# A fused two-block forward pass: five residual turns done as products with a diagonal

## What is computed

```python
def _rmsnorm(x, g):
    y = x * lax.rsqrt(jnp.mean(x * x, axis=-1, keepdims=True) + RMS_EPS)
    return y * g

for i in range(2):                                     # first block
    hn = _rmsnorm(x, norm1[i])
    mix, q_mem = mixer[i](hn, ...)
    x = x + concat([mix, mem_attention(q_mem, ...)]) @ w_o[i]
    x = x + swiglu(_rmsnorm(x, norm2[i]), w_ffn_in[i], w_ffn_out[i])
x = _rmsnorm(x, final_norm)
h = rmsnorm(x, mix_pre_g)                              # second block
merged = ...                                           # from h @ w_in
x = x + rmsnorm(merged @ w_out, mix_post_g)
x = x + rmsnorm(swiglu(rmsnorm(x, ffn_pre_g), ...), ffn_post_g)
```

## Time and profile before

| | |
|---|---|
| runs, us | 1379.44 median, 1378.86 to 1386.27 |
| the profiled execution, us | 1386.25 |
| its span from first to last instruction, us | 1384.5 |
| PE busy | 1260.3 us, 91% of the span |
| DVE busy | 746.5 us, 54% |
| ACT busy | 601.2 us, 43% |
| mean granted PE clock | 0.945 of full speed |
| DMA moved | 184.59 MB, mean 133 GB/s |

### The profile page before, as it was taken

One profiled execution on the slowest core, in us unless ns is written; L12 is line 12 of the kernel. 1 busy time (PEld: TensorE's weight loads), 2 busy tenths in 40 slices (PEclk: granted clock), 3 DMA queues, 4 the chain that ended last, 5 costly groups with the idle time before them and its releaser, 6 DMA issues.

```text
span 1384.5 us, 21989 instructions
## 1 busy us (share of the span) xinstructions
PE 1260.3 (91%) x9316; PEld 1167.7 (84%) x9316; DVE 746.5 (54%) x1207; ACT 601.2 (43%) x983; POOL 57.4 (4%) x44
## 2 busy tenths in 40 slices
PE   5999998999989987989878999979999977799996
PEld 5998878999879677978758999869998866799985
DVE  5556536555454776444455655464645445655544
ACT  5556435444446521212323544435533753444432
POOL 0000000000000023304000000000000000000000
PEclk9999889999999998989989999998999988899998
DMA  9722126666554220000035866554554333366651
GB/s 276 204 92 92 62 65 166 192 184 188 203 161 132 92 91 1 1 2 1 1 113 164 225 183 185 197 166 123 183 183 153 122 122 91 109 188 187 188 184 59
DMA packets 222365, 184.59 MB, mean 133 GB/s; under 512 B 19338, under 2 KB 208016, under 8 KB 222140
## 3 DMA queue, kind: packets, MB, share of 16 engines
q1 hardware_dynamic: 221082, 181.50, 43.7%
q10 hardware_dynamic: 1186, 1.69, 0.4%
HBM read 182.12 MB, written 1.05 MB: 132 GB/s over the span
## 4 chain that ended last, share of the span: by engine, by line
PE 80%; DVE 11%; ACT 4%; issue 2%; DMA 2%; SPq 1%; ACTq 0%; DVEq 0%
PE bank L724 21%; PE bank L726 21%; PE bank L725 21%; PE bank L945 2%; PE bank L819 2%; PE bank L953 2%; DVE w_lo L1846 2%; PE bank L957 2%; ACT w_hi L1443 1%; PE bank L1147 1%; DVE arena L2232 1%; SPq L664 1%; DMA ring<-in_w_ffn_in 1%; PE bank L1131 1%; PE bank L1123 1%
## 5 line engine op out<-in xcount | busy, mean ns | idle before, releaser
L1846 DVE TENSOR_TENSOR w_lo<-ring,w_hi 128x1024 fp32r<-128x1024 f32 (+1 forms) x326 | 383.1, 1217 | 446.9 <-ACT w_hi L1443 446.9
L1443 ACT ACTIVATE w_hi<-ring 128x1024 fp32r<-128x1024 f32 (+1 forms) x326 | 323.3, 1040 | 442.1 <-PE bank L726 420.3
L724 PE MATMUL bank<-act_hi,w_hi 128*128 128x256 f32 (+1 forms) x1512 | 428.4, 283 | 3.2 <-DVE w_lo L1846 1.8
L726 PE MATMUL bank<-act_hi,w_lo 128*128 128x256 f32 (+1 forms) x1512 | 424.8, 281 | 0.0
L725 PE MATMUL bank<-act_lo,w_hi 128*128 128x256 f32 (+1 forms) x1512 | 424.7, 281 | 0.0
L724 PEld LDWEIGHTS bank<-act_hi,w_hi 128*128 128x128 f32 (+1 forms) x1512 | 285.4, 189 | 6.7 <-issue 3.4
L726 PEld LDWEIGHTS bank<-act_hi,w_lo 128*128 128x128 f32 (+1 forms) x1512 | 285.6, 189 | 0.2
L725 PEld LDWEIGHTS bank<-act_lo,w_hi 128*128 128x128 f32 (+1 forms) x1512 | 285.5, 189 | 0.2
L724 PE MATMUL bank<-w_hi,act_hi 128*128 128x256 f32 (+1 forms) x448 | 138.9, 310 | 5.5 <-DVE act_lo L2310 4.2
L725 PE MATMUL bank<-w_lo,act_hi 128*128 128x256 f32 (+1 forms) x448 | 137.0, 306 | 0.0
L726 PE MATMUL bank<-w_hi,act_lo 128*128 128x256 f32 (+1 forms) x448 | 136.5, 305 | 0.0
(11 more groups left out here) (298 smaller groups left out, 1468.7 us busy)
## 6 DMA issues: line engine op xcount, KB each, us to landing
ring<-in_w_ffn_in SPq DMA_DIRECT2D x88, 512.0 KB, 5.2
ring<-in_w_in SPq DMA_DIRECT2D x28, 1024.0 KB, 5.2
ring<-in_w_ffn_out SPq DMA_DIRECT2D x22, 1024.0 KB, 4.9
ring<-in_rw_w_in SPq DMA_DIRECT2D x11, 1024.0 KB, 5.3
ring<-in_w_gate SPq DMA_DIRECT2D x22, 512.0 KB, 4.0
ring<-in_w_up SPq DMA_DIRECT2D x22, 512.0 KB, 5.3
ring<-in_w_down SPq DMA_DIRECT2D x11, 1024.0 KB, 4.8
ring<-in_w_o SPq DMA_DIRECT2D x8, 1024.0 KB, 4.9
```

Of the source, the lines that this page charges most:

```text
L724: pe.matmul(o, ahl[0], bhl[0], start=first, stop=False)
L726: return pe.matmul(o, ahl[1], bhl[0], start=False, stop=final)
L1443: act.activation(w_hi[:, (m % SPLITS) * SLOT + lo:(m % SPLITS) * SLOT + hi], ring[:, r * SLOT + lo:r * SLOT + hi], copy).then_inc(tick(own ...
L1846: dve.tensor_tensor(w_lo[:, c], ring[:, r * SLOT + lo:r * SLOT + hi], w_hi[:, c].bitcast(F32), ALU.subtract).then_inc(tick(own, "lo_ready" ...
```

## The change

At the five sites `scale_rows` no longer scales rows. It multiplies the 128x128 identity by the two columns of inverse norms, into `diagonal`, which lies in the first 256 columns of `sbuf_s`. `to_fm` then takes the 16 tiles of `x_tm` itself as the stationary operand and the diagonal as the moving one: x-transposed times the diagonal is the turned, scaled tile. The other four calls of `to_fm` keep the transposition.

```diff
+    diagonal = sbuf_s[:, 0:2 * P].rearrange("p (q t) -> p q t", q=QT)

-        def to_fm(ready, value):
+        def to_fm(ready, value, scaled=None):
...
                         k = 2 * j + a
-                        src = tm[:, qt, k * P:(k + 1) * P]
-                        ins = pe.transpose(bank[4 + j][:, a * S + qt * P:a * S + (qt + 1) * P], src, ident)
+                        o = bank[4 + j][:, a * S + qt * P:a * S + (qt + 1) * P]
+                        if scaled is None:
+                            ins = pe.transpose(o, tm[:, qt, k * P:(k + 1) * P], ident)
+                        else:
+                            ins = pe.matmul(o, scaled[:, qt, k * P:(k + 1) * P], diagonal[:, qt, :], start=True, stop=True)

-        to_fm("tm_ready", 3)
+        to_fm("tm_ready", 3, x_tm)
...   (the same for 4, 5, 6 and 8)

         def scale_rows(r, src, dst):
             inverse(r)
             for qt in range(QT):
-                ins = dve.tensor_scalar(dst[:, qt, :], src[:, qt, :], rms[:, r, qt:qt + 1], None, ALU.mult)
+                if dst is None:
+                    ins = dve.tensor_scalar(diagonal[:, qt, :], ident, rms[:, r, qt:qt + 1], None, ALU.mult)
+                else:
+                    ins = dve.tensor_scalar(dst[:, qt, :], src[:, qt, :], rms[:, r, qt:qt + 1], None, ALU.mult)
             ins.then_inc(tick(own, "tm_ready"), 1)

-        rms_norm(2, x_tm, tm)
+        rms_norm(2, x_tm, None)
...   (the same for 3, 4, 6 and 8)
```

More of the change, by code:

```diff
@@ L1201, in _ @@
             row_unit("wo0_", j, 4, fm)
-        to_fm("tm_ready", 3)
+        to_fm("tm_ready", 3, x_tm)
         fm_ready()
         ffn("f0")
-        to_fm("tm_ready", 4)
+        to_fm("tm_ready", 4, x_tm)
         fm_ready()
@@ L1302, in _ @@
             row_unit("wo1_", j, 4, fm)
-        to_fm("tm_ready", 5)
+        to_fm("tm_ready", 5, x_tm)
         fm_ready()
@@ L1313, in _ @@
             ins.then_inc(unit_done, 1)
-        to_fm("tm_ready", 6)
+        to_fm("tm_ready", 6, x_tm)
         fm_ready()
@@ L1357, in _ @@
             row_unit("wo2_", j, 4, fm)
-        to_fm("tm_ready", 8)
+        to_fm("tm_ready", 8, x_tm)
         fm_ready()
@@ L2129, in _ @@
         residual("f0_out0", f"f0_out{FT // 2 - 1}")
-        rms_norm(3, x_tm, tm)
+        rms_norm(3, x_tm, None)
         ahead("f0_out10")
@@ L2314, in _ @@
         residual("wo1_0", "wo1_3")
-        rms_norm(4, x_tm, tm)
+        rms_norm(4, x_tm, None)
         ahead("wo1_3")
@@ L2329, in _ @@
                                        C("tri").unsqueeze(1).to_broadcast((P, 4, P)), ALU.mult).then_inc(freed(own, f"wsT{j}"), 1)
-        rms_norm(6, x_tm, tm)
+        rms_norm(6, x_tm, None)
         ahead("f1_out10")
@@ L2414, in _ @@
         dve.wait_ge(*last(own))
-        rms_norm(8, x_tm, tm)
+        rms_norm(8, x_tm, None)
         ahead("wo2_3")
```

## The result

The changed kernel took a median of 1390.43 us (1383.73 to 1395.41, 20 runs) against 1384.61 us (1376.32 to 1388.27, 20 runs) of the kernel before. The ratio is 1.0048, with a 95% interval from 1.0033 to 1.0063: slower, by 5.8 us between the medians. The forecast was 4.1 us faster, at 1375.3 us, in a range of 1369 to 1382. The profiled execution of the changed kernel took 1392.01 us.

The account below looks back on a forecast made before the run. PE was taken as the bound, idle at the sites until DVE's scaling was done. Savings of 0.58 + 0.94 + 3 x 0.87 = 4.1 us, exchange at nothing, gave 1379.44 - 4.1 = 1375.3 us, range 1369 to 1382.

Parts of the forecast that it names:

- The scalings: On DVE at each site, two 128x128 instructions replace two of 128x1024: 0.48 us for 1.42, 0.94 us saved.
- what reached the first product: At the next part's first product: 0.58 us earlier at wo0, 0.94 at f0, 0.87 at wo1, f1 and wo2.
- The turns against the products: On PE at each site, 16 products replace 16 transpositions at no cost, plus or minus 0.16 us a site.
- Rival D: In the run of 16 at each site, a product costs four times a transposition: 1425 us; chance 0.04.
- The clock: After each gap PE works at 0.50; sum 2.4 us if the rise stays, 4.1 if it moves; 4.1 taken.
- Rival B: At four sites the next part's products find full clock: total gain 7.3 us, 1372.2 us; chance 0.20.
- Rival C: In the attention and recurrence parts, half-clock stretches fall longer: 1382 us, slower than before by 0.2%; chance 0.14.
- Rival E: At all sites DVE's saving is eaten by the wait for `w_hi` and by half clock: 1379 us; chance 0.02.
- The level: For the whole kernel, the forecast started from the median of three runs of before, 1379.44 us.

Follow-up runs that it names:

- the kernel with the product alone: Kernel before, DVE's row scalings kept, with a plain f32 product with the identity in place of each transposition at the five sites: 1396.10 us, ratio 1.0073.
- the kernel with DVE's part alone: Changed kernel with the short DVE scalings, but PE turns the residual tiles by transposition with the plain identity: 1382.77 us against 1385.42, ratio 0.9976.

## Why the prediction was wrong

*The scalings.* Right. 0.48 us for the pair, 0.94 us saved, a gap of 3.80 us; what reached the first product (0.58 at wo0, 0.80 to 0.81 where 0.87 was said, more than 0.94 at f0) was confirmed by the kernel that has that part alone.

*The turns against the products.* This is the step that failed. "I cost the exchange at nothing" rested on the earlier trace rows: eight records of L953 in 1.06 us, 0.112 us from start to start, as against 0.113 for a transposition. The spacing was read rightly, but it was the spacing of records, and I took a record for a product. Line L953 stands in a loop of 2 x 5 x 3 x 4 = 120 products, and the trace of the kernel before has 160 + 80 = 240 records on it:

```profile
L953 PE MATMUL bank<-arena x160: 275/275/275, 553.7 to 666.4; 128*128 128x128 f32 x160
L953 PE MATMUL bank<-arena,zshift x80: 275/275/275, 557.2 to 667.3; 128*128 128x128 f32 x80
```

So the price of a plain product was in the trace of before: 2 x 0.112 = 0.224 us at full clock, and by L945 2 x 0.206 = 0.41 at half. Measured were 0.225 and 0.427. With 0.225 - 0.113 and 0.427 - 0.213 the term is 0.11 to 0.21 us per product, 1.8 to 3.4 us per site, not nothing; the kernel with the product alone shows 2.0 to 2.8. Against 0.94 saved that makes a site 0.9 to 2.5 us worse, and the table above shows 0.68 to 2.01. It is less at wo1 because there the clock rose 2.9 us into the longer run, while before all of the run was at 0.50.

*Rival D.* It named the cause, the place and the point from which it decides (0.054 us over a transposition; measured 0.213 at half clock), and it had a chance of 0.04. Its price was off, because it took a factor of four. Two times would have given 16 x 0.208 = 3.3 us a site, 5 x 3.3 - 4.1 = 12 us slower; what was measured is half of that, for the reason in the next point. The factor of four comes from the Trainium skill, "TensorE: Matmul & The Clock Gate" (Terms); here the factor is two, in records and in time. The advice of the Trainium skill, "Perfetto Trace Analysis" (Transposes), to keep a transposition a transposition, was right for this kernel as it stood, and I had argued it away with the miscounted rows.

*The clock.* The prediction left it out of the sum and took it for a lottery. In part it is one: at wo1 the run after had a mean of 0.71, at f0 nearly all of it was at 0.50. But it also acts against the loss. In this pair of profiles the rise to 1.00 came 3.8 to 5.8 us behind the start of the run before and 2.9 to 5.4 us behind it after. Before, the products of the next part spent the end of that time at 0.50; after, the longer run does, and the products find full clock. So 7.4 us at the first products had shrunk to 4.4 by the 144th.

*Rival B* expected full clock for the next part's products because the gap is shorter. The products did find it more often, after runs of 4.9 to 6.2 us, and it was bought with these runs. Shorter gaps alone did little: with 3.8 us the clock still fell at wo0, f0 and wo1. That products in place of transpositions bring the rise is not shown either: the times just given overlap, and in the kernel with DVE's part alone the clock rose at wo1 when PE had run nothing but transpositions since its gap:

```profile
733.53:736.36 2.83, 2.83 (x14) 2.83 (x15) 2.63 (x3) 2.79 (x6) 0.00 (x0) 0.50 0.00 0
736.36:736.98 0.62, 0.49 (x4) 0.28 (x4) 0.62 (x3) 0.60 (x3) 0.00 (x0) 1.00 0.00 0
```

*Rival C* can't explain a difference between medians of 20 runs each with an interval of 1.0033 to 1.0063. *Rival E* is refuted by the kernel with DVE's part alone.

*The level.* The three runs of before that I had were at the low end: their median of 1379.44 became 1384.61 over 20. Even the right sum from there, 1379.4 + 5.8 = 1385.2, would have been 5 us under the measured time. The profiled execution (1386.25) was nearer the middle than that median. Of the 20 runs of before, 17 lie over 1382 us, the top of the stated range, so even no change at all would have fallen outside it.

*What stays open.* How much of the 5.8 us is the sites' and how much the rest, where the clock falls differently in each execution, was not settled closer than 4.4 us at the sites in one pair of profiles.

## What to carry to other kernels

Before you price an operation by the rows of another, divide its records by the number that the source issues; a count that is twice the loop's means that the unit you compare is half of an operation. In float32 a turn by a transposition that has an operand scaled beforehand can be cheaper than a product that does both, if PE's queue is the last to be ready at the site, so price both queues and ask which one the first product behind waits for. Where PE stands idle for some microseconds and then has a short serial run in front of it, see at which clock that run goes: filling the gap with products of no use took 3 us off the kernel before and about 0.8%, 11 us, off the changed one (ratios of 1.0048 and 0.9964 to the kernel before), while the shorter scaling alone was worth 3 us.

## What the runs showed of the hardware

- A plain f32 product 128x128 by 128x128 is two instructions on PE, each with a weight load; a transposition of the same tile is one. 160 records for 80 products, 80 for 80 transpositions, from the same residual rows. 0.225 us against 0.113 at full clock, 0.427 against 0.213 at half.
- A shorter idle stretch of PE didn't keep the clock: after 3.80 us without work it stood at 0.50 at wo0, f0 and wo1 of the changed kernel, as after 4.74 us in the kernel before (at wo0 of before 0.3 us into the run). With 26 to 92 products in the gaps it stayed at 1.00 through the run at all five sites.
- The mean granted clock over the span went from 0.945 to 0.956 and 0.957 with the fill, with 268 and 228 added products of 0.118 us each, all of which lie in time that was idle. Over all executions the ranges are 0.935 to 0.947 without the fill and 0.953 to 0.959 with it.
- The clock rose to 1.00 within a run of nothing but float32 transpositions: at wo1 of the kernel with DVE's part alone, 2.83 us into the run, after an idle stretch of 3.81 us.
